# Two transformer blocks on one core: value products moved into the next weight block, modulation multiply-adds one at a time, and the second unit's weights landing in another buffer

## What is computed

```python
ada = (c @ w_ada + b_ada)                       # 6 rows of 1024: shift1, scale1, gate1, shift2, scale2, gate2
h = rmsnorm(x, g_norm1) * (1.0 + scale1) + shift1
proj = h @ w_in                                 # q,k,v of 8 "fox" heads, forget logits, q,k,v of 8 "dsa" heads,
                                                # q_idx, k_idx, w_idx, two gates of 1024
y_fox = forgetting_attention(...)               # causal, 8 heads of 64
y_dsa = indexer_sparse_attention(...)           # 64 best keys of each query, bias table by distance, 8 heads of 64
merged = sigmoid(gate_fox) * (y_fox @ w_branch_fox) + sigmoid(gate_dsa) * (y_dsa @ w_branch_dsa)
x = x + gate1 * (merged @ w_out)                # then the mlp with shift2, scale2, gate2, rmsnorm
# second block: swiglu, MoBA attention (8 heads of 128), swiglu, swiglu, pool mixer, swiglu, with layer norms
```

## Time and profile before

| what | value |
|---|---|
| time, median of 3 runs | 1419.74 us (1419.46 to 1419.94) |
| the profiled execution's own time | 1418.88 us |
| its span | 1416.9 us |
| PE busy | 1349.1 us (95%), 6233 matmuls |
| DVE, ACT, POOL busy | 824.7, 661.4, 78.4 us |
| mean granted clock of PE | 0.990 |
| chain that ended last | PE 85%, DVE 5%, ACT 3%, DMA 3%, issue 2%, POOL 1% |

### The profile page before, as it was taken

How to read it: one execution, slowest core, us unless ns; L and a number is a source line. 1 busy time by engine, 2 the same in 40 slices (tenths; PEclk the granted TensorE clock), 3 DMA queues, 4 the chain that set the end, 5 groups by cost and what they waited for, 6 DMA issues and landing times.

```text
span 1416.9 us, 16267 instructions
## 1 busy us (share of the span) xinstructions
PE 1349.1 (95%) x6233; PEld 1102.1 (78%) x6233; DVE 824.7 (58%) x1118; ACT 661.4 (47%) x1052; POOL 78.4 (6%) x112
## 2 busy tenths in 40 slices
PE   2899997999999999999998999999999999999997
PEld 2777775878888888888776888888888888888885
DVE  5585664876564755357445755457554575765454
ACT  3566454454353544344555544344443444454442
POOL 3400010000000100000000000001000010100000
PEclk9899998999999999999999999999999999999999
DMA  8745673456644565655631754656655545565551
GB/s 307 266 142 201 221 252 138 148 190 228 226 187 179 185 201 190 196 179 179 217 140 64 231 199 165 199 192 207 202 192 177 205 157 189 193 199 199 174 195 65
DMA packets 156684, 268.37 MB, mean 189 GB/s; under 512 B 9445, under 2 KB 101685, under 8 KB 155584
## 3 DMA queue, kind: packets, MB, share of 16 engines
q1 hardware_dynamic: 148928, 239.45, 49.2%
q0 software_dynamic: 7680, 27.89, 5.9%
HBM read 266.21 MB, written 1.07 MB: 189 GB/s over the span
## 4 chain that ended last, share of the span: by engine, by line
PE 85%; DVE 5%; ACT 3%; DMA 3%; issue 2%; POOL 1%; SPq 0%; DVEq 0%; ACTq 0%; POOLq 0%
PE UP L653 16%; PE UP L655 16%; PE UP L654 16%; PE Y L653 10%; PE Y L655 10%; PE Y L654 10%; PE TB L723 4%; DVE WL L1333 2%; DMA PIECE<-in_w_ada 1%; DMA X<-in_x 1%; ACT WH L1009 1%; DVE ADA L1509 1%; POOL RS L585 1%; POOL VAR L584 1%; PE TB L964 1%
## 5 line engine op out<-in xcount | busy, mean ns | idle before, releaser
L1333 DVE TENSOR_TENSOR WL<-RAW,WH 128x1024 fp32r<-128x1024 f32 (+2 forms) x448 | 514.8, 1194 | 186.6 <-ACT WH L1009 180.7
L1009 ACT CAST WH<-RAW 128x1024 fp32r<-128x1024 f32 (+2 forms) x448 | 436.8, 1033 | 226.5 <-PE Y L655 124.8
L653 PE MATMUL UP<-WH,AH 128*128 128x512 f32 (+1 forms) x1104 | 444.0, 402 | 5.3 <-DVE WL L1333 2.7
L655 PE MATMUL UP<-WH,AL 128*128 128x512 f32 (+1 forms) x1104 | 432.4, 392 | 0.0
L654 PE MATMUL UP<-WL,AH 128*128 128x512 f32 (+1 forms) x1104 | 431.5, 391 | 0.0
L653 PEld LDWEIGHTS UP<-WH,AH 128*128 128x128 f32 x1104 | 209.1, 189 | 49.1 <-issue 7.0
L655 PEld LDWEIGHTS UP<-WH,AL 128*128 128x128 f32 x1104 | 208.9, 189 | 43.9
L654 PEld LDWEIGHTS UP<-WL,AH 128*128 128x128 f32 x1104 | 209.5, 190 | 40.1 <-issue 0.7
L653 PE MATMUL Y<-WH,HH 128*128 128x512 f32 (+1 forms) x496 | 193.6, 390 | 0.0
L655 PE MATMUL Y<-WH,HL 128*128 128x512 f32 (+1 forms) x496 | 191.6, 386 | 0.0
L654 PE MATMUL Y<-WL,HH 128*128 128x512 f32 (+1 forms) x496 | 191.5, 386 | 0.0
(11 more groups left out here) (207 smaller groups left out, 912.3 us busy)
## 6 DMA issues: line engine op xcount, KB each, us to landing
RAW<-in_ffn_w_gu SPq DMA_DIRECT2D x176, 512.0 KB, 4.9
RAW<-in_ffn_w_down SPq DMA_DIRECT2D x80, 512.0 KB, 4.1
RAW<-in_w_mlp SPq DMA_DIRECT2D x64, 512.0 KB, 4.4
RAW<-in_w_in SPq DMA_DIRECT2D x40, 512.0 KB, 5.2
PIECE<-in_w_ada POOLq DMA_DIRECT2D x32, 512.0 KB, 4.2
RAW<-in_a_w_in SPq DMA_DIRECT2D x24, 512.0 KB, 4.6
WADA<-in_w_ada SPq DMA_DIRECT2D x7, 1024.0 KB, 10.1
RAW<-in_w_out SPq DMA_DIRECT2D x8, 512.0 KB, 3.7
```

Of the source, the lines that this page charges most:

```text
L653: pe.matmul(dst, ah, wh, start=first, stop=False)
L655: return pe.matmul(dst, al, wh, start=False, stop=last)
L1009: act.copy(WH[:, u % 2, q * n:(q + 1) * n], RAW[:, q // 2, (q % 2) * n:(q % 2 + 1) * n]).then_inc(wh_done, 1)
L1333: ve.tensor_tensor(WL[:, u % 2, o], RAW[:, q // 2, (q % 2) * n:(q % 2 + 1) * n], WH[:, u % 2, o].bitcast(F32), ALU.subtract).then_inc(wl_d ...
```

## The change

Four things are edited, all in the first 11 units but for one in the MoBA stage. (1) The first half of unit 1 lands in `TAB`'s space, with a semaphore of its own, and SP doesn't wait for it; SP issues the first half of unit 2 when half 0 of unit 0 is split, and POOL reads the bias table only after unit 1's first half is split. (2) In unit 0 ACT rounds two quarters of unit 1 ahead of each block's copy, where it rounded all four ahead of the first; DVE splits two quarters, does the forget logits of the first block, and then the other two. (3) `values` of a head moves from its slot into the next block, behind the second tile (`k == 2`), and ACT's `outputs` moves with it to the next block, behind `round_unit`; the same for four MoBA heads. (4) In units 4 to 10 one piece of modulation is used ahead of the first slot, one behind it and the rest behind the second, and one of the 24 pieces moves from unit 10 to unit 3; in the drain PE waits for the 24 pieces behind the scores.

```diff
--- before.py
+++ after.py
@@ -59,7 +59,7 @@
 WINDOWS = (2, 4, 8, 16)
-MODULATION = (2, 0, 1, 0, 3, 3, 3, 3, 3, 3, 3)
+MODULATION = (2, 0, 1, 1, 3, 3, 3, 3, 3, 3, 2)
 PIECES = sum(MODULATION)
@@ -302,6 +302,7 @@
         ROWCOL = TMP[0:32, 0, 0:P]
+        RAW1 = TAB[:, :, :].rearrange("p a b -> p (a b)")
         XT = PIECE[:, :, :].rearrange("p a b -> p (a b)").rearrange("p (k n) -> p k n", n=256)
@@ -321,6 +322,7 @@
         raw_in = [sem("raw_in0"), sem("raw_in1")]
+        raw1_in = sem("raw1_in")
         wh_done = sem("wh_done")
@@ -424,6 +426,16 @@
+        def raw_half(u, half):
+            return RAW1 if (u, half) == (1, 0) else RAW[:, half, :]
+        def raw_landed(u, half):
+            if (u, half) == (1, 0):
+                return raw1_in, 32
+            return raw_in[half], 32 * (u if half == 0 and u > 1 else u + 1)
         def emptied(b):
@@ -486,10 +498,10 @@
                 for half in range(2):
-                    if u:
-                        sp.wait_ge(wl_done, 4 * u - 2 + 2 * half)
+                    if u and (u, half) != (1, 0):
+                        sp.wait_ge(wl_done, 2 if (u, half) == (2, 0) else 4 * u - 2 + 2 * half)
                     n = width * kts // 2
-                    dst = RAW[:, half, 0:n]
+                    dst = raw_half(u, half)[:, 0:n]
                     if name[0] == "misc":
@@ -523,7 +535,7 @@
                     for dd, ss in parts:
-                        sp.dma_start(dd, ss).then_inc(raw_in[half], 16)
+                        sp.dma_start(dd, ss).then_inc(raw_landed(u, half)[0], 16)
@@ -572,6 +584,7 @@
                 gp.wait_ge(rev_out, 16 * (n + 1))
+                gp.wait_ge(wl_done, 6)
                 start = REVD[n, 0, 0:1]
@@ -663,7 +676,7 @@
-            def wide(u, tok, chain=None, turns=None):
+            def wide(u, tok, chain=None, turns=None, head=None):
@@ -675,6 +688,8 @@
                         ready((chain, tok, k // 4))
+                    if head is not None and k == 2:
+                        values(head)
                     if turns and k == 5:
@@ -771,16 +786,13 @@
-            def slot(a, first, end, sums=()):
+            def slot(a, first, end):
...
                     score(a)
-                for c in sums:
-                    ada_sum(c, c - 4)
-                if first < a <= end:
-                    values(a - 1)
+                return a - 1 if first < a <= end else None
@@ -822,16 +834,17 @@
             late = []
+            head = None
             for u in range(11):
                 name = UNITS[u][0]
-                wide(u, 0)
+                wide(u, 0, head=head)
                 for key, n in late:
...
                 if u >= 4:
-                    slot(att, 0, 2 * NF)
+                    head = slot(att, 0, 2 * NF)
                     att += 1
-                wide(u, 1)
+                wide(u, 1, head=head)
                 if name[0] in ("misc", "qd", "kd", "qf", "kf"):
@@ -854,12 +867,15 @@
                 if u >= 4:
-                    slot(att, 0, 2 * NF)
+                    head = slot(att, 0, 2 * NF)
                     att += 1
-            pe.wait_ge(piece_used, PIECES)
+            values(head)
             while att <= 2 * NF:
-                c = 4 + 2 * (att - 2 * NF + 2)
-                slot(att, 0, 2 * NF, (c, c + 1))
+                head = slot(att, 0, 2 * NF)
+                pe.wait_ge(piece_used, PIECES)
+                for c in (4 + 2 * (att - 14), 5 + 2 * (att - 14)):
+                    ada_sum(c, c - 4)
+                values(head)
                 att += 1
@@ -921,9 +937,12 @@
             att = 2 * NF
+            head = None
             for n, (u, tok) in enumerate(blk for blk in WIDES if UNITS[blk[0]][0][0] == "moba"):
                 i, c = n // 2, UNITS[u][0][1]
-                wide(u, tok, ("f", 0) if n < 4 else None, (("f", 0), 1, X) if n == 1 else None)
+                wide(u, tok, ("f", 0) if n < 4 else None, (("f", 0), 1, X) if n == 1 else None, head)
+                if i >= 5 and head is not None:
+                    head = None
                 if n == 1:
@@ -933,10 +952,10 @@
                 if i >= 3 and (tok == 0 or att < 2 * NF + 4):
-                    slot(att, 2 * NF, 2 * NF + MH)
+                    head = slot(att, 2 * NF, 2 * NF + MH)
                     att += 1
             while att <= 2 * NF + MH:
-                slot(att, 2 * NF, 2 * NF + MH)
+                values(slot(att, 2 * NF, 2 * NF + MH))
                 att += 1
@@ -1005,8 +1024,8 @@
                     if q % 2 == 0:
-                        act.wait_ge(raw_in[q // 2], 32 * (u + 1))
-                    act.copy(WH[:, u % 2, q * n:(q + 1) * n], RAW[:, q // 2, (q % 2) * n:(q % 2 + 1) * n]
+                        act.wait_ge(*raw_landed(u, q // 2))
+                    act.copy(WH[:, u % 2, q * n:(q + 1) * n], raw_half(u, q // 2)[:, (q % 2) * n:(q % 2 + 1) * n]
                              ).then_inc(wh_done, 1)
@@ -1102,8 +1121,7 @@
                     probs(a)
-                if first < a <= end:
-                    outputs(a - 1)
+                return a - 1 if first < a <= end else None
@@ -1132,12 +1150,17 @@
             att = 0
+            head = None
             places = {"qd": QD, "kd": KD, "qf": QF, "kf": KF}
...
                 for tok in range(TOK):
-                    if tok == 0:
+                    if u == 0:
+                        round_unit(1, (0, 1) if tok == 0 else (2, 3))
+                    elif tok == 0:
                         round_unit(u + 1)
+                    if head is not None:
+                        outputs(head)
                     before = UNITS[u - 1][0][0] if u else None
@@ -1190,10 +1213,11 @@
                     if u >= 4:
-                        slot(att, 0, 2 * NF)
+                        head = slot(att, 0, 2 * NF)
                         att += 1
+            outputs(head)
             while att <= 2 * NF:
-                slot(att, 0, 2 * NF)
+                outputs(slot(att, 0, 2 * NF))
                 if att < 2 * NF:
@@ -1280,10 +1308,10 @@
                 if i >= 3 and (tok == 0 or att < 2 * NF + 4):
-                    slot(att, 2 * NF, 2 * NF + MH)
+                    head = slot(att, 2 * NF, 2 * NF + MH)
                     att += 1
             while att <= 2 * NF + MH:
-                slot(att, 2 * NF, 2 * NF + MH)
+                outputs(slot(att, 2 * NF, 2 * NF + MH))
                 att += 1
@@ -1330,7 +1358,7 @@
                     o = slice(q * n, (q + 1) * n)
-                    ve.tensor_tensor(WL[:, u % 2, o], RAW[:, q // 2, (q % 2) * n:(q % 2 + 1) * n],
+                    ve.tensor_tensor(WL[:, u % 2, o], raw_half(u, q // 2)[:, (q % 2) * n:(q % 2 + 1) * n],
                                      WH[:, u % 2, o].bitcast(F32), ALU.subtract).then_inc(wl_done, 1)
@@ -1549,18 +1577,19 @@
             for u in range(11):
-                split_unit(u + 1)
+                split_unit(u + 1, (0, 1) if u == 0 else range(4))
...
                     forget_out(0)
+                    split_unit(1, (2, 3))
+                    forget_in(1)
+                    forget_out(1)
                 if u >= 4:
+                    modulation(1)
                     slot(att, 0, 2 * NF)
                     att += 1
-                if u == 0:
-                    forget_in(1)
-                    forget_out(1)
+                    modulation(1)
                 if u == 1:
@@ -1573,13 +1602,10 @@
                     table_ready(0)
-                if u == 10:
-                    modulation(MODULATION[u])
                 if u >= 4:
...
                     att += 1
-                if u < 10:
-                    modulation(MODULATION[u])
+                modulation(MODULATION[u] - (2 if u >= 4 else 0))
             while att <= 2 * NF:
...
                 c = 4 + 2 * (att - 2 * NF + 2)
```

## The result

The changed kernel takes 1399.94 us (median of 4 runs, 1398.17 to 1401.90); the kernel before, run beside it on the same chip, 1419.60 us (4 runs, 1418.91 to 1419.94). The ratio is 0.986, with a 95% interval of 0.9849 to 0.9872. On another chip the same two gave 1398.32 and 1419.41 us, ratio 0.9849 (0.9836 to 0.9863). The forecast was 1402.5 us with a range of 1398.5 to 1407.

What follows compares the result with a forecast made beforehand. The prediction took PE's work plus its standstill and half clock to bound the kernel. Savings of 5.2 (start), 0.7 (values), 1.7 (pieces) and 9.7 (drain) made 17.3 us, so 1402.5 us was forecast, range 1398.5 to 1407.

Steps and rivals of the forecast that it cites:

- the four places named: PE's waits at unit 1's start, for probabilities before values, for exponentials before turn_probs, and 7.95 us ahead of the drain.
- Start: Units 1 and 2: unit 1 starts at 48.2 us at full clock, unit 2 at 66.1 instead of 71.27; 5.2 us saved.
- the wait ahead of unit 2: Before unit 2's transposes: PE waits 2.1 us for ACT's copy, which stands behind rounding unit 2's second half.
- Values: Values moved into the next block: 2.3 us of waits go, 1.6 us lost to cuts; net 0.7, between -0.9 and 2.3.
- 16 x 0.1 = 1.6 us lost: Blocks cut by moved values, 12 groups here and 4 in the MoBA stage: each cut costs 0.1 us.
- Pieces: Units 4 to 10: using pieces one at a time ends waits for exponentials; net 1.7 us saved, between 1.0 and 2.1.
- The new wait in unit 4: Unit 4: two more pieces (2.6 us) ahead of the first maxima, against 2.3 us of slack; 0.4 us lost.
- Drain: Two drain slots: 6.9 us go with the piece wait, 2.8 us through full clock; 9.7 saved, between 8 and 10.5.
- (a): Rival: the clock falls in the new 2.1 us wait before unit 2; time 1404 to 1405.5 us; 22%.
- (b): Rival: three softmax chains hold the clock low in the drain, whose 9.7 us becomes 5; time 1407 us; 8%.
- (c): Rival: the change does nothing, the piece wait moving to a later piece or PE finding another late; 2%.
- (d): Rival: slower, as outputs behind ACT's rounding delay the next values in each of 7 units; 1420 to 1425 us; 2%.

Runs made afterwards that it cites:

- start_order: The kernel before with only ACT's and DVE's new order in unit 0, unit 1's first half landing as before: 1418.04 us, ratio 0.9986.
- wait_behind: The kernel before with only PE's wait for the 24th piece moved behind the scores of each drain slot: 1420.57 us, ratio 1.0003.
- pieces_order: The kernel before with only DVE's new order of pieces and one piece moved from unit 10 to unit 3: 1409.09 us, ratio 0.9920.
- values_back: The changed kernel with values and outputs back in their own slots: 1403.16 us, ratio 0.9878.
- start_again: The changed kernel with ACT's copies of two blocks ahead of roundings and DVE's second forget logits taken in ahead of a split: 1396.81 us, ratio 0.9844.
- norm_order: The changed kernel with DVE scaling each norm's second half straight behind its centring, the weight quarter split after it: 1404.75 us, ratio 0.9892.
- best: The changed kernel with dummy matmuls only where PE waits in the drains, plus the edit of start_again: 1394.54 us, ratio 0.9822.

## Why the prediction was right, and where it was not

**What bounds the kernel.** Right in the main: the four places named gave 20.7 us, nearly all of it standstill and half clock. Some 0.7 us of the values' gain is no wait but closer packing of the same matmuls, which the prediction had with the opposite sign. The MoBA stage gave 0.75 us and unit 0 0.5, and clock and POOL took 3.2 us back.

**Start.** The mechanism was right: unit 1 at 47.32 (48.2 forecast) at full clock, one wait of 1.37 us for the second forget logits (1.3), one for ACT's copy. The term was 5.2 us and measured 6.2, or 6.7 with the 0.5 us of unit 0. What was mis-sized is the transfer of unit 2's second half, "issued behind that same split, at 52.1, and takes 8.4 us", carried over from before: it took 6.9 (7.2 in the second profile), which made the wait ahead of unit 2 0.63 us instead of 2.1. I had this as a bound ("the second may land 1 us sooner (6.2)"), and start_order shows the 8.6 us back again when the first half is issued late.

**Values.** The step that failed is "the first matmul of a run takes 0.33 us", and with it "16 x 0.1 = 1.6 us lost": a cut costs 0.03 us at most in slots 5 to 7 and saves some 0.15 in the five slots behind them. In units 4 to 10 the values gave 2.6 us, four waits of 0.5 and the rest from the later slots; the MoBA stage, whose waits I had not counted, gave three times 0.36 and lost 0.32 in a fourth slot. Net 3.3 where I took 0.7 and allowed 2.3 at most: the bound was wrong too, since it held no gain beyond the waits.

**Pieces.** 2.0 us against 1.7. The new wait in unit 4 came, 0.5 us against 0.4. What I did not see is that the values' gain depends on this part: alone they gain 0.6 us up to the drain.

**Drain.** 7.06 and 2.87 us against 6.9 and 2.8, from the same two slots, and the wait ahead of head 13's turn is 0.94 us for 1.3. I read the 7.95 us as PE's wait for the 24th piece. It is DVE's: in wait_behind PE doesn't wait for the piece and stands 8.40 us for head 13's exponentials all the same. wait_behind and pieces_order show that DVE's new list of pieces did it all, and the place of PE's wait nothing; how much of it is their order and how much the piece that left unit 10 is open.

**Rivals.** (a), the clock in the new wait before unit 2, didn't come; start_order had 2.36 us there without it. (b) came in part and at another place: 1.5 us in the deep block behind the drain, in one profile of two. The Trainium skill (TensorE: Matmul & The Clock Gate, "What's actually happening") says that the gate runs free of the kernel, so that the moment of a switch varies. The trace agrees: the same instructions at the same place ran at 0.50 once and at 1.00 once. (c) and (d) didn't show: outputs behind the rounding never made PE wait.

**The sum.** 17.3 was forecast, 19.0 came (1418.88 less 1399.87). The errors were +1.0 and +0.5 at the start, +2.6 for the values, +0.3 for the pieces, +0.2 in the drain, and against them -1.5 by the clock and -1.7 by POOL, about 1.4 us in all, the rest is rounding. So it is partly luck that the total came out so near: the last two nearly hid that the values were mis-sized by a factor of more than four, and without the experiments the total would have looked like a confirmation of each term.

## What to carry to other kernels

When two engines share an in-order chain, an early transfer is worth nothing while the consumer's copy stands behind a later transfer on the same engine: change the order first (4.1 us here, at the start of unit 2), then the landing place (2.1 more). Price a move at both ends: what the moved instructions cost where they were against where they go, not only the cut they make. And where a wait is named "issue" or by a semaphore, look at what the engine behind the next operand was doing; moving the wait itself changed nothing here.

## What the hardware showed that I had not expected

The granted clock did not follow the length of a wait. It stayed at 1.00 through 2.36 us of standstill in start_order, and fell to its lower level behind two waits of 0.32 and 0.47 us in pieces_order; values_back had those two waits too and kept it. Between two profiles of one kernel a stretch of 6 us differed by 1.5 us for this reason alone. Dummy matmuls in the waits kept the clock at 1.00 in both drains in all three kernels that had them, and the mean clock was 0.997 to 0.999 in all 12 of their executions. Without them it was 0.994 to 0.998 in the 21 executions of the changed kernel and its other variants, and only start_again's profile kept 1.00 through and behind the MoBA drain, so the dummies make a fall rarer and are not the only way to be spared it.

POOL's 128x1 operations took 0.30 to 2.67 us. In the second half of each late norm they had two outcomes: 0.30 to 0.49 us for `VAR` and 0.84 for `RS`, or 0.79 to 1.07 and 1.42 to 1.51. In the long case above `VAR` ends 0.08 us after DVE's pair of 128x512 operations, and `RS` 0.42 us after DVE's split. In the short case `VAR` ends 0.17 us after the first of the pair, and `RS` 0.42 us after the second. With DVE idle in norm_order `RS` took 0.56. Of the five late norms two were long in the kernel before, two to five in the five kernels that are before with one part changed, five in the changed kernel, four in its second profile and none in best. Where one turned long PE lost 0.5 us on the next weights. The Trainium skill (SBUF — State Buffer, "SBUF: two separate sides") calls the port pair of the two engines an exclusive lock that whoever starts first holds for the whole instruction, against a DVE operation with two inputs in SBUF. The trace agrees: by the numbers above POOL's operation ends behind one of DVE's each time that DVE is at work. Why one execution gets the short turn and another the long one wasn't settled: in the two cases shown DVE's pair starts 0.43 and 0.42 us ahead of `VAR`.
